# Decoder layer on 8 cores: a new order for the second half of the cross-attention, and the last tile's norm product on GpSimd

## The reference, cut to what matters

```python
x = x + merged @ w_out[l]                    # token mixers before this are left out here
# memory cross-attention: 4 heads of 128, 256 memory tokens
hc = rms_norm(x, ln_cross_w[l])
qc = (hc @ wq_cross[l]).reshape(B, S, CROSS_HEADS, HEAD_DIM)
sc = jnp.einsum('bshd,bmhd->bhsm', qc, kvc[:, :, 0]).astype(jnp.float32) * (HEAD_DIM ** -0.5)
pc = jax.nn.softmax(sc, axis=-1).astype(x.dtype)
oc = jnp.einsum('bhsm,bmhd->bshd', pc, kvc[:, :, 1]).reshape(B, S, CROSS_WIDTH)
x = x + oc @ wo_cross[l]
# SwiGLU channel mixer
hf = rms_norm(x, ln_ffn_w[l])
x = x + (jax.nn.silu(hf @ w1[l]) * (hf @ w3[l])) @ w2[l]
return rms_norm(x, ln_final_w)
```

## Time and profile before

| what | us |
|---|---|
| median of 3 runs (2279.42 to 2527.74) | 2282.6 |
| the profiled execution | 2280.11 |
| its span on the slowest core (core 6) | 2278.4 |
| spans of the 8 cores | 2273.4 to 2278.4 |
| PE busy | 2205.7 (97% of the span) |
| DVE busy | 802.0 (35%) |
| ACT busy | 562.6 (25%) |
| POOL busy | 179.9 (8%) |
| mean granted clock of PE, by core | 0.994 to 0.997 of full |

### The profile page before, as it was taken

The page is one execution under the profiler, slowest core; times in us unless marked ns, Lnnn a source line. Parts: engine busy times, 40 slices in busy tenths (PEclk is TensorE's granted clock), DMA queues, the critical chain, the costliest instruction groups (busy, mean ns, idle before and its releaser), DMA issues.

```text
span 2278.4 us, 36013 instructions; the slowest of 8 cores (2273.4 to 2278.4 us)
## 1 busy us (share of the span) xinstructions
PE 2205.7 (97%) x14656; PEld 1188.7 (52%) x14656; DVE 802.0 (35%) x1287; ACT 562.6 (25%) x939; POOL 179.9 (8%) x217
## 2 busy tenths in 40 slices
PE   4899999999999999999999989999999999999998
PEld 2676766766656664444444444444444444444443
DVE  2543222245555552111113462224324314414416
ACT  3442111145555552111112562000000000000014
POOL 0000000001011112222210000000000000000000
PEclk9999999999999999999999999999999999999999
DMA  9754453130431408363695317444444444444323
GB/s 230 180 142 75 75 88 52 30 57 2 74 54 22 70 5 172 52 102 51 99 188 79 75 19 148 74 74 74 74 74 75 74 75 75 74 84 80 70 45 148
DMA packets 61616, 188.72 MB, mean 83 GB/s; under 512 B 3472, under 2 KB 36240, under 8 KB 45456
## 3 DMA queue, kind: packets, MB, share of 16 engines
q0 software_dynamic: 53968, 145.01, 38.4%
q1 hardware_dynamic: 7488, 41.43, 5.2%
HBM read 323.04 MB, written 8.39 MB: 145 GB/s over the span
## 4 chain that ended last, share of the span: by engine, by line
PE 87%; DVE 6%; ACT 4%; issue 2%; DMA 1%; DVEq 0%; SPq 0%; ACTq 0%
PE P L306 86%; DVE hU L899 1%; DMA R<-xo 1%; DVE R L897 1%; DVE R L808 1%; PE P L372 1%; ACT R L804 1%; PE P L1089 1%; DVE R L839 0%; ACT L804 0%; DVE R L361 0%; ACT L763 0%; DVE R L814 0%; ACT R L357 0%; DVE R L802 0%
## 5 line engine op out<-in xcount | busy, mean ns | idle before, releaser
L306 PE MATMUL P<-hT,wb 128*128 128x512 bf16 (+1 forms) x6016 | 1328.3, 378 | 2.2 <-DVE hT L317 1.4
L306 PEld LDWEIGHTS P<-hT,wb 128*128 128x128 bf16 x6016 | 580.6, 98 | 671.1 <-issue 7.4
L306 PE MATMUL P<-wb,hT 128*128 128x128 bf16 (+1 forms) x6464 | 717.4, 272 | 5.6 <-DVE R L317 2.9
L306 PEld LDWEIGHTS P<-wb,hT 128*128 128x128 bf16 x6464 | 462.6, 108 | 256.5 <-issue 7.1
L1054 DVE TENSOR_TENSOR R<-R,P 128x512 f32<-128x512 f32 x384 | 262.7, 687 | 151.7 <-PE P L306 150.8
L1269 DVE TENSOR_TENSOR hT<-P,tmp 128x512 bf16<-128x512 f32 x88 | 60.9, 692 | 538.2 <-PE P L306 538.2
L1268 ACT ACTIVATE tmp<-P 128x512 f32<-128x512 f32 x88 | 52.5, 597 | 782.0 <-PE P L306 781.9
L1010 DVE TENSOR_TENSOR tmp<-P,R 128x512 f32<-128x512 f32 x64 | 44.3, 691 | 246.7 <-PE P L306 246.7
L285 POOL DMA_DIRECT2D wb<-w x66 | 39.3, 596 | 905.5 <-PE P L306 895.2
L994 ACT ACTIVATE R<-P 128x512 f32<-128x512 f32 x64 | 38.2, 597 | 249.7 <-PE P L306 249.7
L306 PE MATMUL P<-R,wb 128*128 128x512 bf16 (+1 forms) x448 | 95.9, 365 | 0.0
(11 more groups left out here) (116 smaller groups left out, 989.7 us busy)
## 6 DMA issues: line engine op xcount, KB each, us to landing
wb<-w POOLq DMA_DIRECT2D x66, 1024.0 KB, 10.9
wb<-w_in POOLq DMA_DIRECT2D x50, 1024.0 KB, 15.1
R<-xo SPq DMA_DIRECT2D x16, 1024.0 KB, 12.9
R<-xp SPq DMA_DIRECT2D x8, 1024.0 KB, 6.3
wb<-w_out POOLq DMA_DIRECT2D x8, 1024.0 KB, 19.4
y<-R SPq DMA_DIRECT2D x14, 512.0 KB, 2.8
wb<-wkv_c POOLq DMA_DIRECT2D x4, 1024.0 KB, 15.4
wb<-w_bb POOLq DMA_DIRECT2D x8, 512.0 KB, 9.6
```

The source lines that it names most:

```text
L306: P.pe(lambda e: e.matmul(out, lhsT, rhs, start=start, stop=stop, skip_group_check=skip), reads=reads, writes=writes)
```

## The change

In the first hunk the same calls stand in another order: c_score and c_pv of the second half's heads 0 to 3 are spread behind wo_tile(0) to wo_tile(3), one head at a time, hn_tr(0) stands behind wo_tile(1) and before q_proj(3, 1), and hn_tr(1) before hn_scale(3). The order of q_proj and wo_tile among themselves is as before, and so are the banks that they take.

In the second hunk, the first three pieces of tile 7 are multiplied by the row of norm weights on GpSimd as soon as they have been squared. After rstd_x(7), ACT scales columns 0 to 1023 by the norm, DVE does the last piece as before (norm and weights in one) and scales columns 1024 to 1535; three stores (512, 512 and 1024 columns) take the place of four of 512.

```diff
         wo_tile(0)
+        c_score(0, 1, (2, 3))
         q_proj(2, 1)
+        c_pv(0, 1)
         wo_tile(1)
+        c_score(1, 1, (2, 3))
+        hn_tr(0)
         q_proj(3, 1)
-        c_score(0, 1, (2, 3))
+        c_pv(1, 1)
         wo_tile(2)
-        c_pv(0, 1)
-        c_score(1, 1, (2, 3))
+        c_score(2, 1, (2, 3))
         wo_tile(3)
-        c_pv(1, 1)
-        c_score(2, 1, (2, 3))
+        c_pv(2, 1)
         rstd_x(3, 2)
+        c_score(3, 1, (2, 3))
+        hn_tr(1)
         hn_scale(3)
-        hn_tr(0)
-        hn_tr(1)
-        c_pv(2, 1)
-        c_score(3, 1, (2, 3))
         hn_tr(2)
         c_pv(3, 1)
         hn_tr(3)
...
                 sq_x(t, nb)
+                if t == 7 and nb < 3:
+                    xr = xs[:, 7, nb * 512:(nb + 1) * 512]
+                    P.pool(lambda e, xr=xr, nb=nb: e.tensor_tensor(out=xr, in0=xr, in1=rowf[:, nb * 512:(nb + 1) * 512], op=ALU.mult),
+                           reads=[("x", 7, nb), "rowf"], writes=[("x", 7, nb)])
                 if t > 0:
...
         rstd_x(7)
-        for i in range(4):
-            store(7, i * 512, 512)
+        r7 = rsv[:, 7:8]
+        P.act(lambda e: e.activation(out=xs[:, 7, 0:1024], in_=xs[:, 7, 0:1024], func=AF.Copy, scale=r7),
+              reads=[("x", 7, 0), ("x", 7, 1), ("rs", 7)], writes=[("x", 7, 0), ("x", 7, 1)])
+        store(7, 1536, 512)
+        P.dve(lambda e: e.tensor_scalar(out=xs[:, 7, 1024:1536], in0=xs[:, 7, 1024:1536], scalar1=r7, scalar2=None, op0=ALU.mult),
+              reads=[("x", 7, 2), ("rs", 7)], writes=[("x", 7, 2)])
+        for c0, n in ((1024, 512), (0, 1024)):
+            ks = [("x", 7, i) for i in range(c0 // 512, (c0 + n) // 512)]
+            P.dma("sp", lambda e, c0=c0, n=n: e.dma_start(out=y[7 * 128:8 * 128, c0:c0 + n], in_=xs[:, 7, c0:c0 + n]),
+                  reads=ks, writes=[("y", 7, c0)])
```

## The result

| | before | changed |
|---|---|---|
| median of 15 runs each | 2282.27 | 2307.37 |
| lowest, highest | 2279.42, 2527.74 | 2280.28, 2712.34 |
| changed / before | | 1.0057, 95% interval 1.0032 to 1.0082 |

What follows compares the result with a forecast made beforehand. TensorE, busy 2205.7 of 2278.4 us, was taken as the bound. Cross-attention order +3.2 and tail +0.8 gave +4.0 on the profiled 2280.1: 2284.1 us, range 2279.0 to 2288.0.

Steps and rivals of the forecast that it cites:

- first stall: Cross-attention: TensorE waits at hn_tr(0) for DVE's hn_scale(0), a new idle of 3.0 us.
- its clock: Work at half clock behind each cross-attention stall: 1.3 us lost after the first, 1.9 after the second.
- second stall: Cross-attention: TensorE waits at hn_tr(2) for ACT's copy of hn_tr(1) out of bank 6, 5.8 us idle.
- c_score(0,1) to wo_tile(4): Reordered cross-attention stretch: 26.0 us of work plus both stalls and their clock losses, 38.0 us against 34.85.
- stage, changed less before: Net cost of the first hunk's new order in the cross-attention: +3.2 us, from +1.3 to +3.9.
- last addition later by: Tail: POOL's products and DVE's scales of tile 6 shut each other out, delaying the last addition 1.0 us.
- stores: End of the kernel: fewer, larger pieces of the final output gain 0.2 us, bounds -0.3 and 0.
- base: Time the sum was added to: the profiled execution's 2280.1 us, with the median of the runs shown at 2282.6.
- The walk: Cross-attention: earlier trace's durations laid out in the new order on PE, ACT and DVE; hn_tr(0) resumes at 1314.8, hn_tr(2) at 1336.6.
- The rival in which the gap closes: Cross-attention: hn_tr(1)'s copy is done by about 1331, when PE reaches hn_tr(2); 2274 us; chance 0.15.
- The milder rival: Cross-attention: first stall leaves the clock alone, second costs 1.3 in clock, tail gives -0.2; 2281.2 us; chance 0.20.
- The rival "the clock stays low": Low clock lasts into the FFN for over 90 us, costing 46 us; chance 0.02.

Runs made afterwards that it cites:

- the third order: Kernel before, cross-attention reordered: c_score of heads 0 and 1 between first wo tiles, q_proj(3,1) held back; 2273.59 us (0.9961), on another chip 2275.43 (0.9964).

## Why the prediction was right in its steps and wrong in its number

| step | predicted | measured |
|---|---|---|
| first stall, released by DVE L1079, in issue time | 3.0 | 3.04 (idle 2.88) |
| its clock | 1.3 | 1.4 (0.77 in the transposes, 0.60 in q_proj), up to 1.7 on other cores |
| second stall, released by ACT L315, in issue time | 5.8 | 6.07 (idle 5.91) |
| its clock | 1.9 | 2.2 (0.78, 0.85 and 0.58), up to 2.6 on other cores |
| c_score(0,1) to wo_tile(4) | 38.0 | 38.70 |
| stage, changed less before | +3.2 | +3.8 |
| last addition later by | 1.0 | 0.93 |
| stores | -0.2 | -0.3 to -0.5 |
| sum, by the undisturbed cores | +4.0 | +5.1, +5.2, +4.4 in the last three sessions |
| base | 2280.1 | 2282.3 to 2283.4 |
| median of runs with no core low | 2284.1 | 2287.0, 2287.7, 2286.8, 2287.5 |
| median as measured | 2284.1 | 2307.37 |

**The walk was right.** Laid over the trace with the 4.76 us by which this stretch starts earlier (1298.38 against 1303.14), the walk's release of hn_tr(0) at 1314.8 falls on 1310.04; the trace has 1310.06. Its start of hn_tr(2), 1336.6, falls on 1331.84; the trace has 1332.23, 0.4 later. Of this 0.1 is the first stall's clock. The other 0.3 came in on ACT: its cast of q_proj(3,1) starts 4.58 after that group, where the walk took 3.71 and the half clock explains 0.60 of the rest; every step of DVE and ACT behind it up to the copy is late by as much. No run shows why. That the cure of one queue (PE's) would be paid in another (ACT's) came out of nothing but the durations of the earlier trace rows. The rival in which the gap closes fell at its own test, the copy's end: it had to be about 1331 and came at 1332.08 + 4.76 = 1336.8.

**Terms that were mis-sized.** The two for the clock, taken from one earlier gap and from the rest of the work in the stretch: 3.2 predicted, 3.6 to 4.3 measured, by core. With them and the 0.3 of the second stall the stretch came to 38.70, +3.85, just under the upper bound of +3.9. The milder rival, in which the first stall leaves the clock alone, did not come true on any core here (q_proj(3,1) took 4.05 to 4.88 us on them, for its 3.45). But it isn't wrong as a mechanism: of the 56 cores in the seven profiles that have this stall, three kept the full clock through it, with the same 2.88 us of idle. One is core 6 of the changed kernel's run on chip 2 (PE's timeline), where the granted clock is 1.00 throughout and the stage 1.2 us shorter than the others' median:

```profile
1316.54 1.05 PE L1089 MATMUL P<-cb,hT 128*128 128x128 bf16 x16 [2.88 <-DVE hT L1079]
1317.42 3.62 PE L306 MATMUL P<-hT,wb 128*128 128x512 bf16 x15
```

**The tail.** The scales' 1.79 and 1.69 against 1.8 and 1.8, and the addition's 0.93 against 1.0, rested on one pair of rows from a far stage, where a DVE instruction of 0.69 ended 0.54 after POOL's. Here one of 1.28 ended 1.09 after it: in both it is nearly its own length, less 0.15 to 0.20 (the walk took 0.15). The run without POOL's products shows the cause. The rule of the Trainium skill (SBUF — State Buffer, "Who interferes with whom") held in both directions: POOL's second product took 1.88 and its third 1.78, beside 1.26 for its first, which had begun before DVE's scale. The transfer stayed without a pause:

```profile
2301.50:2304.50 3.00, 0.00 (x0) 0.00 (x0) 0.00 (x0) 0.00 (x0) 0.00 (x0) 0.50 0.99 339
```

**What failed, first: the base.** The sum was laid on the profiled execution, 2280.1, while the runs' median was 2282.6 and is 2282.3 to 2283.4 in every later session. The slowest of eight cores is a draw from a scatter (the kernel before's undisturbed cores lie between 2271 and 2283 from run to run), and one low draw was taken for the mean. The step "I count from 2280.1" lost 2 to 3 us. With it put right the same sum gives 2286.3 to 2287.4, and the undisturbed medians are 2286.8 to 2287.7. As it stood, the range held them by only 0.3 to 1.2 us.

**Second, and this is the 23 us: a lasting fall of the clock, which the sum and its range put at nothing.** The rival "the clock stays low" was given 0.02, with "nothing in the trace shows more than some 7 us", and priced at 46 us by the half clock alone. Something like it happened in 6 of 15 runs, at another level (0.81), on two cores of eight, and, in the one of them that was profiled, for 161 us: 27 us in place of none. Since that is 6 of 15, and 2 more were long with a whole half low, the median itself fell on it; in the next session of this kernel 5 of 12 had it and the median was 2298, in the two after that none of 20 and the medians were 2287.0 and 2287.5. That this kernel's first 15 runs fell in such a session is bad luck for the number; that the range had no room for it is not. The trace of before had shown eight cores that never did this in one execution; the step from one execution to "0.02" was not a reading of rows. One number of before did speak against it: of its three runs one took 2527.7 us, so that this chip's clock, or something like it, was disturbed in a third of what was shown, and the range had no room for a small portion of that. Its size, 27 us, no row of before could give. A chance of its own for a disturbed slowest core, and a range open to the top by it, would have been the right form; the steps of the sum would have stayed as they are.

## What to carry to other kernels

When heads or tiles are spread along an in-order program, walk every engine's queue, not PE's: a PSUM bank is free only when the engine that copies it out reaches the copy, and what is moved in between them (two exponentials, 1.06 us) is paid nearly one to one by TensorE: 5.67 us more of stall made the stage 5.1 longer. The clock is paid on top once for a stall (2.2 to 2.6 us behind 5.91, no more behind 11.58). Put behind each other what the copying engine must do first: the third order of the same calls makes it 0.9961 and 0.9964 of before. Lay a small sum on the median of the runs, not on the profiled execution; and give a time that is the slowest of eight cores a range that a disturbance of two of them can fill.

## What the runs showed of the hardware

- The granted clock of PE has a third level here beside half and full: 0.81, held for 158 to 161 us each of the three times that a profile has it, by two neighbouring cores at once (4 and 5, or 6 and 7), while the other cores of the same half, with the same load, stayed at full. By the Trainium skill (TensorE: Matmul & The Clock Gate, "Seeing it yourself", the warning "Peak-current limiter: 13/16 clock (1.95 GHz) once three cores of a die run dense matmuls") the level is 13/16 and it is the whole die's for as long as the load lasts. The level agrees (0.81), and a few runs fit the rest: one of the kernel before took 2709.5 us with four cores at a mean of 0.813 to 0.814. Most runs don't: in them all eight cores, with PE busy for about 97% of 2.28 ms, kept a mean of 0.993 or more, and what fell in the changed kernel's profile was a pair, once, for 161 us.
- Filling a gap of TensorE with matmuls whose result is thrown away took away the half clock behind it: with 39 matmuls in two gaps the stage was 2.3 us shorter.
- A stall of 2.9 us on TensorE cost another 1.4 to 1.7 in the work behind it on 53 of 56 cores and nothing on three; one of 5.9 cost another 2.2 to 2.6.
- A DVE instruction of two SBUF operands that meets a POOL product ends its own length less 0.15 to 0.20 us after POOL's, whether it is 512 or 1024 wide (0.69 and 1.28 us long by itself); POOL's product of 1.26 took 1.78 and 1.88 when DVE's was already running.
